# Spatial gating between the second and third projection of the odd layer, its bias added by VectorE, the second projection evacuated by ScalarE

## What is computed

```python
def sgu_mixer(xm, w_in, ln_g, ln_b, w_sp, b_sp):
    u, v, z = jnp.split(xm @ w_in, 3, axis=-1)
    v = layer_norm(v, ln_g, ln_b)
    vh = v.reshape(bsz, nc, SGU_CHUNK, N_SGU_HEADS, SGU_HEAD_DIM)
    s = jnp.einsum('hts,bnshc->bnthc', w_sp, vh) + b_sp.T[None, None, :, :, None]
    return u * s.reshape(bsz, seqlen, D_SGU) * jax.nn.silu(z)
```

## Time and profile before

| | |
|---|---|
| median of 3 timed runs | 4363.92 us (4361.32 to 4364.85) |
| span of the profiled execution | 4368.1 us |
| the profiled execution's own time | not given apart from its span |
| PE busy | 3910.7 us, 90% |
| weight loads of PE | 3717.4 us, 85% |
| GpSimd busy | 3110.1 us, 71% |
| VectorE busy | 1792.1 us, 41% |
| ScalarE busy | 1609.7 us, 37% |
| HBM read | 709.37 MB, 163 GB/s |

### The profile page before, as it was taken

One profiled execution on the slowest core, in us unless ns is written; L12 is line 12 of the kernel. 1 busy time (PEld: TensorE's weight loads), 2 busy tenths in 40 slices (PEclk: granted clock), 3 DMA queues, 4 the chain that ended last, 5 costly groups with the idle time before them and its releaser, 6 DMA issues.

```text
span 4368.1 us, 78341 instructions
## 1 busy us (share of the span) xinstructions
PE 3910.7 (90%) x31206; PEld 3717.4 (85%) x31206; DVE 1792.1 (41%) x2279; ACT 1609.7 (37%) x2267; POOL 3110.1 (71%) x1292
## 2 busy tenths in 40 slices
PE   9699996878998899989998999957999999399987
PEld 1599995878987888979998999947999999399986
DVE  0667357844023244263024294175443000944433
ACT  0212432233323333354443344454444444544442
POOL 0357960856755664868888798878887888788864
PEclk9799997989978999999999999968999999599998
DMA  9366740733433442535544455513554555045532
GB/s 348 120 241 262 268 184 1 283 129 137 173 115 109 142 151 88 186 132 188 188 164 154 178 180 182 185 45 125 182 185 173 190 182 185 7 164 182 186 143 97
DMA packets 98368, 713.80 MB, mean 163 GB/s; under 512 B 11040, under 2 KB 11168, under 8 KB 12064
## 3 DMA queue, kind: packets, MB, share of 16 engines
q1 hardware_dynamic: 97344, 705.75, 44.6%
q10 hardware_dynamic: 864, 5.76, 0.3%
HBM read 709.37 MB, written 2.10 MB: 163 GB/s over the span
## 4 chain that ended last, share of the span: by engine, by line
PE 71%; DVE 15%; issue 6%; POOL 5%; ACT 2%; DMA 1%; DVEq 1%; POOLq 0%; ACTq 0%; SPq 0%
PE bank L473 48%; PE bank L841 17%; POOL unit_lo L420 5%; PE bank L534 2%; DVE hot L1854 1%; DMA ring<-in_w 1%; DVE peer_w L1868 1%; PE bank L520 1%; DVE log_a L1745 1%; DVE hot L1861 1%; DVE ada_acc L1167 1%; DVE rms_tmp L1610 1%; PE bank L626 1%; DVE v1f L1577 1%; PE bank L608 1%
## 5 line engine op out<-in xcount | busy, mean ns | idle before, releaser
L420 POOL TENSOR_TENSOR unit_lo<-ring,unit_hi 128x1024 fp32r<-128x1024 f32 x1140 | 2870.9, 2534 | 871.9 <-ACT unit_hi L865 871.0
L473 PE MATMUL bank<-xl_hi,unit_hi 128*128 128x256 f32 x5696 | 1616.2, 284 | 152.1 <-POOL unit_lo L420 57.0
L865 ACT ACTIVATE unit_hi<-ring 128x1024 fp32r<-128x1024 f32 x1140 | 1175.0, 1056 | 1384.1 <-PE bank L473 589.7
L473 PE MATMUL bank<-xl_lo,unit_hi 128*128 128x256 f32 x5696 | 1605.6, 282 | 0.0
L473 PE MATMUL bank<-xl_hi,unit_lo 128*128 128x256 f32 x5696 | 1604.9, 282 | 0.0
L473 PEld LDWEIGHTS bank<-xl_hi,unit_hi 128*128 128x128 f32 x5696 | 1085.8, 191 | 166.9 <-issue 68.9
L473 PEld LDWEIGHTS bank<-xl_lo,unit_hi 128*128 128x128 f32 x5696 | 1085.7, 191 | 0.1
L473 PEld LDWEIGHTS bank<-xl_hi,unit_lo 128*128 128x128 f32 x5696 | 1085.1, 191 | 0.0
L841 PE MATMUL bank<-w_r,unit_hi 128*128 128x256 f32 x4096 | 727.8, 280 | 6.9 <-DVE w_r L1892 6.9
L841 PEld LDWEIGHTS bank<-w_r,unit_hi 128*128 128x128 f32 x4096 | 628.7, 189 | 7.1 <-issue 7.1
L841 PE MATMUL bank<-w_r,unit_lo 128*128 128x256 f32 x2048 | 574.1, 280 | 0.0
(11 more groups left out here) (363 smaller groups left out, 4371.9 us busy)
## 6 DMA issues: line engine op xcount, KB each, us to landing
ring<-in_w SPq DMA_DIRECT2D x671, 1024.0 KB, 4.8
resid<-in_xT ACTq DMA_DIRECT2D x1, 2048.0 KB, 12.7
tmp_ctx<-in_ctxT ACTq DMA_DIRECT2D x1, 2048.0 KB, 10.7
out<-resid SPq DMA_DIRECT2D x4, 512.0 KB, 2.6
con<-in_con ACTq DMA_DIRECT2D x1, 576.0 KB, 3.3
con<-in_con ACTq DMA_DIRECT2D x1, 448.0 KB, 6.2
p_tmp<-in_pT ACTq DMA_DIRECT2D x1, 256.0 KB, 3.3
vec<-in_vec ACTq DMA_DIRECT2D x1, 246.0 KB, 4.5
```

Source lines behind the costliest of these rows:

```text
L420: pool.tensor_tensor(lb[b][:], ring[slot][:, f * HALF:(f + 1) * HALF], hb[b][:].bitcast(F32), ALU.subtract).then_inc(lo_done, 1)
L473: mm = pe.matmul(bank[(s.t0 + tile[m]) % TILES][:, 0:T], w[b][:, (i % 8) * P:(i % 8 + 1) * P], mv[x][:, k, :], start=(k == 0 and w is hb a ...
L865: act.activation(hb[b][:], ring[slot][:, f * HALF:(f + 1) * HALF], ACT.Copy).then_inc(hi_done, 1)
```

## The change

- In `STAGES`, u1 is marked "A": ScalarE evacuates it with Copy. The unit "wsp" moves ahead of z1's units.
- PE makes the spatial matmuls right after the transposes, before z1. The 32 single-row matmuls are gone. A bank is free again when VectorE has made its addition (`sgu_read`).
- VectorE no longer copies u1. Per chunk it adds `b_sp`, read from SBUF and repeated over both token chunks, to the PSUM tile into a new small buffer `sgu_s` (two of 128 x 256), waits for that, and multiplies u by it. The last addition releases the unit "wsp". Before the loop it waits for ScalarE's last copy of u1. The products with silu(z) then wait for z1's evacuations group by group.

```diff
@@ STAGES
-    ("u1", "NNNN", 4, 1, "D"),
+    ("u1", "NNNN", 4, 1, "A"),
+    ("wsp", "P", 1, 0, "D"),
     ("z1", "NNNN", 4, 1, "A"),
-    ("wsp", "P", 1, 0, "D"),
@@ buffers
+        vst1 = zone("sgu_s", 112, [P, 2, T])
@@ TensorE
-            run("z1", [xl])
-
             w = slot_wait("wsp")
             pe.wait_ge(S("v1_tok"), 8)
             for c in range(KC):
                 b = bank[4 + c % 4]
                 if c >= 4:
-                    pe.wait_ge(S("sgu_used"), c - 3)
+                    pe.wait_ge(S("sgu_read"), c - 3)
                 for t in range(2):
-                    pe.matmul(b[:, t * P:(t + 1) * P], vt1[:, t, c * P:(c + 1) * P], w[:, (c // 2) * P:(c // 2 + 1) * P],
-                              start=True, stop=False, skip_group_check=True)
-                    mm = pe.matmul(b[:, t * P:(t + 1) * P], ones[0:1, :],
-                                   w[0:1, HALF + (c // 2) * P:HALF + (c // 2 + 1) * P], start=False, stop=True,
-                                   skip_group_check=True)
-                mm.then_inc(S("sgu_done") if c < KC - 1 else plain_done, 1)
+                    mm = pe.matmul(b[:, t * P:(t + 1) * P], vt1[:, t, c * P:(c + 1) * P],
+                                   w[:, (c // 2) * P:(c // 2 + 1) * P], start=True, stop=True, skip_group_check=True)
+                mm.then_inc(S("sgu_done"), 1)
+            run("z1", [xl])
             run("out1", [yh])
@@ ScalarE
-            run("u1")
+            run("u1", lambda i, ps: act.activation(at_chunk(uu, i), ps, ACT.Copy))
@@ VectorE
-            run("u1", lambda i, ps, _: dve.tensor_copy(at(uu, i), ps))
             for g in range(8):
                 dve.wait_ge(S("v1_tp"), g + 1)
                 dve.tensor_copy(vt1[:, g // 4, (g % 4) * 512:(g % 4 + 1) * 512], bank[5 + g % 2][:]
                                 ).then_inc(S("v1_tok"), 1)
+            slot_sp = ring[PLAN["wsp"].u0 % RING]
+            dve.wait_ge(tile_free["A"], TILES + PLAN["z1"].ta)
             for c in range(KC):
+                b_sp = slot_sp[:, HALF + (c // 2) * P:HALF + (c // 2 + 1) * P]
+                dve.wait_ge(S("sgu_done"), c + 1)
+                dve.tensor_tensor(vst1[:, c % 2, :].rearrange("p (n t) -> p n t", n=2),
+                                  bank[4 + c % 4][:, 0:T].rearrange("p (n t) -> p n t", n=2), bc(b_sp, 2), ALU.add
+                                  ).then_inc(S("sgu_read") if c < KC - 1 else plain_done, 1)
                 if c < KC - 1:
-                    dve.wait_ge(S("sgu_done"), c + 1)
+                    dve.wait_ge(S("sgu_read"), c + 1)
                 else:
                     dve.wait_ge(plain_done, PLAN["wsp"].p0 + 1)
-                dve.tensor_tensor(uu[:, c, :], uu[:, c, :], bank[4 + c % 4][:, 0:T], ALU.mult
-                                  ).then_inc(S("sgu_used"), 1)
-            dve.wait_ge(S("sgu_used"), KC)
-            dve.wait_ge(tile_free["A"], TILES + PLAN["wsp"].ta)
+                go(dve.tensor_tensor(uu[:, c, :], uu[:, c, :], vst1[:, c % 2, :], ALU.mult))
+            sync()
             for g in range(NG):
+                dve.wait_ge(tile_free["A"], TILES + PLAN["z1"].ta + GR * (g + 1))
                 go(dve.tensor_tensor(group(uu, g), group(uu, g), group(zz, g), ALU.mult))
                 event("y1")
```

## The result

The changed kernel took 4325.25 us in the median of four runs, against 4362.62 us for the kernel before in four; the ratio is 0.9908 (95% interval 0.9891 to 0.9925), a gain of under 1%. Timed again later, in six runs against eleven, it was 4317.20 against 4360.07, ratio 0.9904 (0.9883 to 0.9926). That is 37 to 43 us; 40.2 were forecast. Single executions are far wider apart than the three runs first shown: the kernel before ranged from 4343.7 to 4373.7 us over the later ones.

A forecast was written before the change was run, and what follows sets the result against it. It took PE's stall in u1 behind VectorE's norm and the uncovered gating after z1 as the bounds. Gains 14.0 + 43.6 less 17.4 lost make 40.2 us: median 4363.9 to 4323.7 us, range 4318 to 4337.

The forecast's parts named there:

- part 2: Between u1 and z1: the gating moved ahead of z1 delays z1's start, 17.4 us lost.
- Part 1: In u1: evacuation by ScalarE removes PE's wait for VectorE and some half clock, 14.0 us gained.
- the lower bound of 12.5: Least loss before z1, in us: 0.9 us a chunk, no contention, no clock lost.
- t1: The time of u1's last matmul, from which the forecast counts the gating ahead of z1.
- The contention of 1.0 us: In the gating before z1: one VectorE multiply meets GpSimd's work and is delayed, 1.0 us lost.
- the 2.7 us of half clock: At z1's start: PE idles between pairs in the gating, so z1 begins at the lower clock, 2.7 us lost.
- Part 3: Between z1 and out1: only group 3's product with silu(z) remains after z1, 43.6 us gained.
- (a): In the gating loop: every multiply meets GpSimd, 2.0 us a chunk, 11 us more, 4335 us; chance 0.11.
- (b): In u1: GpSimd can't keep up with the weight halves, 5 to 8 us lost, 4330 us; chance 0.08.
- (c): In the gating loop: clock stays high, 2.7 us less, 4321 us, or 4319 at 0.9 us a chunk; chance 0.04.
- (d): Before the transposes: the layer norm ends after u1 and holds PE; slower if it takes 128 us; chance 0.01.
- (e): After z1: something the old gating covered, such as out1's loads, still holds out1; 4367 us, no change; chance 0.02.

The follow-up runs named there:

- the second profile before: The kernel before, profiled again with no edit; 337.5 us from u1's first matmul to out1's last evacuation, timed median 4360.07 us.
- The second profiles: The kernel before and the changed kernel, each profiled again with no edit; timed medians 4360.07 and 4317.20 us, ratio 0.9904.
- The version spread over units: Changed kernel with v's transposes behind u1's last four units, two gating chunks behind each of z1's first eight; 4310.98 us, ratio 0.9891.

## Why the prediction was right, and where it was not

The first median lay 1.6 us from the forecast, the second 6.5. That the first came so close is luck: part 2 was forecast 5.8 us too dear, and medians of this kernel move by as much. The order of the effects (a stall gone from u1, a smaller loss ahead of z1, a large gain behind it) was right; what the forecast had wrong is why the gating was slow, and so which edit brings the gain.

- **Part 1, 14.0 us: right.** u1 fell by 14.2 between the first profiles, and the evacuation alone, put in or taken out, is worth 13.1 to 14.5 up to out1's start (11.3 against the second profile before, part of whose u1 went at the faster pace). The norm ended at 1065.8, 43.5 us after its first multiply, where four groups of 12.8 were forecast. The groups took 12.4, 8.7, 11.0 and 11.0 us. What I take for the reason is that in a stage emptied by ScalarE GpSimd has pauses, 0.6 to 0.9 us before a unit, in which VectorE gets on; the 8.7 us group has two of them. I had seen such pauses in z1 and not carried them over. No run isolates this. GpSimd's timeline during the norm:

```profile
1021.41 15.56 POOL L421 TENSOR_TENSOR unit_lo<-ring,unit_hi 128x1024 fp32r<-128x1024 f32 x6 [18.20 <-ACT unit_hi L862]
1037.79 4.94 POOL L421 TENSOR_TENSOR unit_lo<-ring,unit_hi 128x1024 fp32r<-128x1024 f32 x2 [0.83 <-ACT unit_hi L862]
1043.61 10.59 POOL L421 TENSOR_TENSOR unit_lo<-ring,unit_hi 128x1024 fp32r<-128x1024 f32 x4 [0.88 <-ACT unit_hi L862]
```

- **Part 2, 17.4 us lost: too much; 11.64,** which is below even the lower bound of 12.5. Three terms of it failed. A chunk took 0.80 us, not 1.0: the multiply starts 0.46 us after the add, and the next add overlaps its end; that made the loop 2.2 us shorter, while its first add came 0.4 later than forecast (t1 + 7.25). The contention of 1.0 us did not come: GpSimd's last low half ended at 1117.27, t1 + 7.7, as forecast, and the first multiply began at 1117.28, no later behind its add than the others. That it missed GpSimd by 0.01 us is luck. And the 2.7 us of half clock did not come: PE waited for VectorE in each chunk from the seventh on and the clock stayed at 1.00. I had carried the fallen clock from the old loop to the new one, but it belonged to the single-row matmuls.
- **The reading of the old gating was wrong.** I wrote that the 32 single-row matmuls were half of the gating, some 18 of its 42 us. Without them it takes 10.5 us, so they made over 31; with full rows in their place it takes 14.2, so 28 of these are the row count alone. Rows such as the earlier trace rows show one fp32 matmul in two instructions, not a pair of matmuls, and its 0.72 us hold the change of form and the half clock. The forecast was not hurt, because the new loop is paced by VectorE.
- **Part 3, 43.6 us: right, 44.0.** Last evacuation of z1 to last of out1: 1217.24 to 1314.88, 97.6 us; the boundary from gr to ro gave 98.0. The second profiles (139.1 and 98.8 us) give 40.3, with the kernel before in its fast out1. Group 3's product took 1.23 us and was hidden.
- **The sum, 40.2.** Up to out1's start the gain is 43.9 to 45.8; in the stretch 46.6 between the first profiles and 40 to 47 with the second ones; in the medians 37 to 43. The 14.2, 11.64 and 44.0 of the first profiles add up to 46.6; the 6.4 us above the forecast are the 5.8 us of part 2 and 0.6 of the others. That the medians show less is the spread between executions, as far as two profiles a kernel can tell.
- **What the forecast did not ask.** It priced the move as a gain of 43.6 against a loss of 17.4. Both are true of the whole change, but the runs divide it otherwise: taken one after the other up to out1's start, from the first profile before, u1's evacuation brings 13.1 (248.2 to 235.1), the bias edit 29.8 (to 205.3) and the move 2.9 (to 202.5). In other orders the bias edit is worth 28.9 (behind z1, u1 by VectorE) or 36.6 (ahead of z1), u1's evacuation 14.0 or 14.5, and the move 2.3, or a loss of 4.0 with the old bias.
- **Rivals.** (a) and (b) didn't happen: adds 0.80 us apart, no PE wait on `unit_lo` in u1. (c), the clock stays up and a chunk takes less, is what happened, with a chunk shorter still than its 0.9. (d) was far: the norm had 44 us left. (e) did not happen: out1 began 4.37 us after z1.

The exclusion that the prediction cites from the Trainium skill (SBUF — State Buffer, section "SBUF: two separate sides") changed nothing in the chunk loop, since GpSimd had just run out of buffers. The version spread over units agrees with it: 1481 ns for two SBUF inputs, 421 with one. The prediction compared 9.47 with 1.38 us for it, but these are scale-and-shifts with one tensor input. The norm's multiply has two, and takes 3.20 us beside GpSimd and, in the kernel before, 1.23 without:

```profile
1050.88 1.23 DVE L1264 TENSOR_TENSOR v1f<-v1f,rstd 128x1024 f32<-128x1024 f32 x1
```

## What to carry to other kernels

Before moving a slow piece of work to a better place, ask why it is slow: here the piece shrank from 42 to 10.5 us where it stood, and then its place mattered by 2 to 3 us; unmended, the move cost 4.0 us. A bias row added by a one-row matmul looks free in arithmetic, but between full matmuls it doubled the time of each matmul and let the clock fall; one elementwise addition was far cheaper. When the same PSUM banks are emptied by an engine that has a long chain of other work, give them to the idle one.

## What the runs showed of the hardware

- Matmuls of 128 rows by 128 columns in fp32 followed each other at 0.22 us; alternating with one-row or 64-row ones, at 0.415, all at clock 1.00 (with one row, until the clock fell).
- A PE that its records show busy throughout (41.92 of 41.96 us) had a clock of 0.50 for 36 us in the alternation with one-row matmuls; a PE that waited for VectorE in each chunk from the seventh on, with full matmuls only, kept 1.00 for the whole loop. With 64 rows in place of one it stayed at 1.00. So the profile's busy share did not tell what the clock would do.
- At clock 1.00, with PE busy throughout, the same 48 matmuls of a unit took 5.65 us in most stages and 5.44 in some, and which stages were fast differed between two profiles of one kernel. A stage of 16 units so differs by 3 us by chance.
- Executions of one kernel differ by 30 us (4343.7 to 4373.7), while z1, where nothing was put between its units, took 84.7 us from its first evacuation to its last in every profile. A change of this size is read more surely from the part that it touches, cut off before the next long stage, than from two medians.
